# Convolution block: the norm's reciprocal deviation made by token in two columns and spread by two diagonal products

## The reference

```python
def layernorm(x, g, b):
    xf = x.astype(jnp.float32)
    mu = jnp.mean(xf, axis=-1, keepdims=True)
    xc = xf - mu
    y = xc * lax.rsqrt(jnp.mean(xc * xc, axis=-1, keepdims=True) + EPS) * g + b
    return y.astype(x.dtype)

def conformer_conv(h, w_in, b_in, w_dw, b_dw, ln_g, ln_b, w_out):
    ...
    y = jax.nn.silu(layernorm(y, ln_g, ln_b))
    return (y @ w_out).astype(h.dtype)
```

## Time and profile before

| | |
|---|---|
| three executions | 941.40, 943.34, 941.03 us; median 941.4 |
| the profiled execution | 941.0 us |
| its span in the trace | 938.9 us |
| PE busy | 908.8 us, 97% of the span |
| DMA | 286 MB, mean 305 GB/s over the span, some 428 GB/s when it is full |

### The profile page before, as it was taken

How to read it: one execution, slowest core, us unless ns; L and a number is a source line. 1 busy time by engine, 2 the same in 40 slices (tenths; PEclk the granted TensorE clock), 3 DMA queues, 4 the chain that set the end, 5 groups by cost and what they waited for, 6 DMA issues and landing times.

```text
span 938.9 us, 13252 instructions
## 1 busy us (share of the span) xinstructions
PE 908.8 (97%) x5218; PEld 537.0 (57%) x5218; DVE 277.9 (30%) x738; ACT 209.6 (22%) x500; POOL 198.7 (21%) x329
## 2 busy tenths in 40 slices
PE   7999999999999999999988999999999999999996
PEld 5788687544434444344433434488756558688544
DVE  2499824310101101011001011234135346250334
ACT  3365624211101111001101001132215511011640
POOL 0188400111111111111101111031003202013221
PEclk9999999999999999999999999999999999999999
DMA  9999975899999999999999999993300942202001
GB/s 349 428 425 419 405 297 203 347 384 431 428 427 429 427 428 424 429 427 428 428 427 429 427 422 425 427 414 140 156 2 19 427 171 114 89 14 77 1 1 45
DMA packets 24682, 286.12 MB, mean 305 GB/s; under 512 B 2738, under 2 KB 3506, under 8 KB 5426
## 3 DMA queue, kind: packets, MB, share of 16 engines
q1 hardware_dynamic: 23904, 283.99, 72.9%
q10 hardware_dynamic: 722, 1.33, 0.4%
HBM read 284.26 MB, written 1.05 MB: 304 GB/s over the span
## 4 chain that ended last, share of the span: by engine, by line
PE 74%; DMA 16%; DVE 6%; SPq 2%; issue 1%; POOL 0%; ACT 0%; POOLq 0%; DVEq 0%
PE bank L1032 18%; PE bank L1296 17%; DMA arena<-in_w_expert_up 10%; PE bank L1313 8%; PE bank L1517 5%; DVE bank L1772 5%; PE bank L1323 4%; DMA arena<-in_w_expert_down 3%; PE bank L1464 3%; DMA arena<-in_w_ada 3%; PE bank L1496 2%; PE bank L1284 2%; PE bank L1530 1%; PE bank L1655 1%; PE bank L1481 1%; PE bank L1044 1%
## 5 line engine op out<-in xcount | busy, mean ns | idle before, releaser
L1296 PE MATMUL bank<-arena 128*64 128x512 f32 x1024 | 226.2, 593 | 11.0 <-DMA arena<-in_w_expert_up 10.8
L1032 PE MATMUL bank<-arena 128*128 128x256 f32 (+1 forms) x992 | 211.1, 373 | 0.6 <-ACT arena L883 0.4
L1032 PEld LDWEIGHTS bank<-arena 128*128 128x128 f32 x992 | 183.2, 190 | 26.7 <-issue 3.0
L1296 PEld LDWEIGHTS bank<-arena 128*64 128x64 f32 x1024 | 75.8, 137 | 155.9 <-issue 154.8
L1313 PE MATMUL bank<-arena 128*64 128x512 f32 x512 | 116.9, 598 | 0.8 <-DVE arena L1963 0.6
L853 ACT ACTIVATE arena<-bank 128x512 f32<-128x512 f32 x32 | 19.1, 598 | 375.6 <-PE bank L1305 375.6
L1967 DVE TENSOR_TENSOR arena<-bank,arena 64x512 f32<-64x512 f32 x32 | 21.8, 683 | 263.5 <-ACT arena L849 263.5
L608 POOL COPY der<-arena 128x4 f32 (+1 forms) x30 | 5.6, 188 | 317.9 <-PE bank L1305 298.3
L1313 PEld LDWEIGHTS bank<-arena 128*64 128x64 f32 x512 | 33.9, 136 | 66.8 <-issue 64.7
L1323 PE MATMUL bank<-arena 64*128 64x256 f32 x512 | 65.8, 386 | 0.6 <-DVE arena L1985 0.5
L1772 DVE SCALAR_TENSOR_TENSOR bank<-arena,par,bank 128x256 f32<-128x256 f32 x143 | 58.3, 482 | 0.6
(11 more groups left out here) (262 smaller groups left out, 847.5 us busy)
## 6 DMA issues: line engine op xcount, KB each, us to landing
arena<-in_w_expert_down SPq DMA_DIRECT2D x29, 2048.0 KB, 30.7
arena<-in_w_expert_up SPq DMA_DIRECT2D x28, 2048.0 KB, 26.6
arena<-in_w_expert_gate SPq DMA_DIRECT2D x27, 2048.0 KB, 28.3
arena<-in_w_ada SPq DMA_DIRECT2D x8, 2048.0 KB, 39.3
arena<-in_w_expert_gate SPq DMA_DIRECT2D x10, 1024.0 KB, 31.5
arena<-in_w_ada SPq DMA_DIRECT2D x8, 1024.0 KB, 17.2
arena<-in_w_expert_up SPq DMA_DIRECT2D x8, 1024.0 KB, 34.3
arena<-in_w_kv SPq DMA_DIRECT2D x4, 2048.0 KB, 10.2
```

Source lines behind the costliest of these rows:

```text
L1032: mm = pe.matmul(bank[part:part + m, at:at + n], w[:, k, lo:lo + m], rhs[:, k0 + k, :], start=(i == 0), stop=(i == tiles - 1))
L1296: mm = pe.matmul(GU_BANK[half * WIN:(half + 1) * WIN, :], xw[b][:, k, :], w[:, k, :], start=(k == 0), stop=(k == KD - 1), skip_group_check ...
```

## The change

The sum of squares is formed the other way round: the squares are the stationary operand and one column of ones the moving one, so that each token's sum comes out on its own partition, 128 tokens in each of two columns. ACT takes the root of these two columns (128x2), and DVE the reciprocal (128x2). DVE then multiplies `ident` with each of the two columns, which gives two diagonal matrices of 128x128, and PE multiplies `ones` with each diagonal, which puts the reciprocal of every token on all partitions again ("rstd1", in bank 5). DVE reads it there. The two new products stand in PE's program between the sum of squares and `ada(8, 2)`, and wait for DVE's diagonals. A wait of the attention block on `rstd_ready` counts one less, since this reciprocal no longer raises it.

```diff
+        token_var, token_rstd = arena[:, R + 13296:R + 13298], arena[:, R + 13300:R + 13302]
+        rstd_diag = area(R, NT, P)
...
         plan("var1", 5)
+        plan("rstd1", 5, readers=0)
...
-            norm_std("var1", D, eps6)
+            bank = filled(act, "var1")
+            act.activation(token_var, bank[:, 0:NT], ACT.Sqrt, bias=eps6, scale=1.0 / D).then_inc(read("var1"), 1)
...
-            act.wait_ge(sem("rstd_ready"), 4)
+            act.wait_ge(sem("rstd_ready"), 3)
...
-            total("var1", sq, KD, lambda k: pe.wait_ge(sem("squared1"), k + 1))
+            bank = may_fill(pe, "var1")
+            for k in range(KD):
+                pe.wait_ge(sem("squared1"), k + 1)
+                for t in range(NT):
+                    mm = pe.matmul(bank[:, t:t + 1], sq[:, k, t * P:(t + 1) * P], ones[:, 0:1], start=(k == t == 0),
+                                   stop=(k == KD - 1), skip_group_check=True)
+            mm.then_inc(full("var1"), 1)
+            bank = may_fill(pe, "rstd1")
+            for t in range(NT):
+                pe.wait_ge(sem("rstd_diag"), t + 1)
+                mm = pe.matmul(bank[:, t * P:(t + 1) * P], ones, rstd_diag[:, t, :], start=(t == 0),
+                               stop=(t == NT - 1), skip_group_check=True)
+            mm.then_inc(full("rstd1"), 1)
             ada(8, 2)
...
-            rstd = rstd_of("var1")
+            moved(dve, "var1")
+            then(dve.reciprocal(token_rstd, token_var))
+            for t in range(NT):
+                dve.tensor_scalar(rstd_diag[:, t, :], ident, token_rstd[:, t:t + 1], None, ALU.mult) \
+                    .then_inc(sem("rstd_diag"), 1)
+            rstd = filled(dve, "rstd1")[:, 0:T]
```

## The result

The changed kernel takes 944.93 us (median of 8 executions, 943.95 to 947.97) against 941.21 us of the kernel before beside it (median of 8). The ratio is 1.0043, 95% interval 1.0033 to 1.0053: 3.7 us slower, where 1.6 us was forecast and the range ended at 944.6. The profiled execution is the longest of the eight, 947.97 us with a span of 946.1, so its steps are read for the mechanism, and what the change costs is taken from the medians.

What follows compares the result with a forecast made beforehand. PE was taken to end last, its delay reaching the end one for one: 0.1 us (sum of squares), 1.1 (idle) and 0.46 (new products) make 1.6, so 943.0 us against the 941.4 median; range 941.3 to 944.6.

Steps and rivals of the forecast that it cites:

- absorbed: Rival, chance 0.13: the loads' slack from 138 to 203 us swallows PE's delay, giving 941.4 us.
- the stand: PE idle between the sum of squares and the first diagonal's product, 113.53 to 114.61 us, forecast at 1.1 us.
- (b) to (d): After the sum of squares: root to reciprocal 0.33 us, reciprocal to first diagonal 0.20, diagonal's start to its product 0.35.
- (e): Two products of 128 columns with the diagonals, ahead of `ada(8, 2)`: 0.23 us each, 0.46 in all.
- The gain of the norm: The norm's gain starts 0.58 us earlier, which was forecast to be worth nothing because `ada(8, 2)` ends later.
- (a): Sum of squares: sixteen one-column products replace eight of 256 columns, 0.234 us each, 3.74 in all, 0.1 dearer.
- The sentence on the clock: At PE's wait for the diagonals: an idle time of that length takes nothing from TensorE's clock.
- slower for certain: Rival, chance 0.13: one-column products in the sum of squares cost 0.33 us each, 1.54 us more; 944.6 us.
- The last rival: Rival, chance 0.04: the norm shortens and the diagonals are ready when PE comes to them; 941 us at best.
- The upper bound of 2.2: Largest delay of `ada(8, 2)`: 1.6 us plus dear ends for root, diagonals and last products (0.28, 0.14, 0.2).

Runs made afterwards that it cites:

- first run: The changed kernel with 128 columns of ones instead of one in each of the sixteen products of the sum of squares; 943.22 us, ratio 1.0021.
- fifth run: The kernel before with sixteen unused products of 128 columns added ahead of its eight products of the sum of squares; 944.23 us, ratio 1.0029.
- third run: The changed kernel with 128 columns in the sum of squares and `ada(8, 2)` cut in halves around the diagonals' products; 941.44 us, ratio 0.9998.
- fourth run: The kernel before with sixteen unused one-column products added ahead of its eight products of the sum of squares; 947.46 us, ratio 1.0067.
- second run: The kernel before with one wait added on PE: `ada(8, 2)` waits until the reciprocal of 256 columns is done; 945.42 us, ratio 1.0040.

## Why the prediction was wrong

**What bounds the kernel: right.** PE ends last at the place of the change, and its delay goes to the end one for one: 6.0 + 1.7 - 0.2 of delay ahead, 7.2 at the end. The rival *absorbed* falls with it. The first and the fifth run speak against it too: their delays of 1.8 and 3.6 us arrived as 1.9 and 2.7 us (0.21% and 0.29%). The third run's 0.8 us is too small to see in its times (-0.02%, interval -0.12% to 0.08%).

**The order, the stand, the diagonals: right.** The stand was 1.1 us as put down, and the first run met each term from (b) to (d) to 0.1 us. Term (e) was 0.2 us short there, at full clock: 115.30 - 114.66 = 0.64 us from the first product with a diagonal to `ada(8, 2)`, where the forecast has 0.44. The gain of the norm was worth nothing: in the first run the gain's multiplications began 115.41 - 109.78 = 5.63 us behind the first load against 6.16 before, and nobody waited for them.

**Step (a) failed.** I took the price of a product from the logits' row at 0.234 us, and that is its price while the clock is up (3.70 us for sixteen in the fourth run). I took the clock for granted, and with it `ada(8, 2)`, which the sum carries at its old 3.65 us. In the changed kernel the clock fell within 1.5 us of the first one-column product, and the sixteen took 5.78 us in the profiled execution.

**The sentence on the clock looked at the wrong thing.** I asked only whether the stand of 1.1 us could bring the clock down, found waits of 2.0 us that had not, and in the first run's profile was right on that. The fall came ahead of the stand, over the one-column products, while PE's record had no gap; with 128 columns in the same places the clock stayed at 1.00, twice. The trace of before held no row against them: over the logits, its narrowest stream of this kind, the clock was 1.00. Term (e) and `ada(8, 2)` then cost 0.7 and 1.6 us more than forecast; 0.2 of the 0.7 is the shortfall of (e) at full clock, and the rest came at the lower clock. Over (a), (e) and `ada(8, 2)` that makes 2.0 + 0.7 + 1.6 = 4.3 of the 4.4 us by which the profiled execution's output products were later than forecast.

**The rival *slower for certain*** had nearly the time (944.6) and nearly the pace (0.33 us a product against 0.36), but by the wrong mechanism: weight loads that nothing hides. The runs refute that, since the same loads stream at full clock. With the right one, the price would also have been laid on what stands behind the sum. That its time came so near is luck.

**Slips in the working that changed nothing.** One output product is 14.05 / 4 = 3.5 us and not 3.4. The last rival would need the root by about 112.65 (113.53 less the 0.88 from root to first diagonal product) and not 112.4. The upper bound of 2.2 leaves out the 1.54 that (a) itself gives; that stands only in the rival.

Between the medians the falls of the clock, the second one with them, cost 2 to 4 us: 0.22% between the changed kernel and the first run, 0.38% and 0.41% in the two other pairs that differ by columns alone. Their size varies from execution to execution: of the changed kernel's eight, the three longest (946.18 to 947.97) have a mean granted clock of 0.992 to 0.993, the other five (943.95 to 944.96) one of 0.994 to 0.996; the profiled execution of before has 0.998.

## What to carry to other kernels

A price taken from a row holds at the granted clock of that row. When an edit swaps wide products for as many or more narrow ones on a busy PE, look at the clock of the stretch and of what stands behind it, and not only at PE's busy share, which is 100% in the rows of the fourth run and of the fifth alike. Widening the moving operand cost nothing here: sixteen products took 3.65 us of loads with 1, with 32 and with 128 columns, at full clock. And a shorter chain was worth nothing where PE ended last: the work that used to cover the chain was queued behind it, and cutting that cover in two, with the wider products, gave back the loss and no more.

## What the runs showed of the hardware

That TensorE's granted clock can fall to 0.50 while its record has no gap: the one-column products of the changed kernel at 110.8 us, and, with PE 100% busy in the rows from 111 to 117 us, the fourth run at about 113.6 us. With 128 columns in place of one there was no such fall. The Trainium skill, "TensorE: Matmul & The Clock Gate", in its part on the clock gate, ties the lower clock to idle stretches between bursts of products. The second run's fall is of that kind (2.5 us of stand, then 0.50), though its stand is shorter than the gap that the page's table of goals names. The fourth run shows a fall that is not of that kind: its one stand, 0.9 us ahead of the added products, is in the kernel before too. A fall also reaches what stands behind it: `ada(8, 2)`, 256 columns a product and without a gap, still ran at 0.50 from 117.62 us in the changed kernel, and the clock came back only near 121. And not every fall is tied to the one-column products: behind the logits the same stretch of work ran at 0.50 in five of the ten profiles and at 1.00 in the other five, and no run says why.
